# A three-block transformer on one NeuronCore: stage boundaries split by halves of the tokens on both sides

## The reference, cut to what matters

```
block 1, layer 0:  ffn -> mlstm -> ffn -> ple          (each: x = x + f * rms(branch(rms(x)*g)) * g')
block 1, layer 1:  shared k,v from x; ffn -> diff attention -> ffn -> ple
block 2:           x = x + mix(rms(x));  x = x + peer_ffn(rms(x))
block 3:           x = x + rms(mix3(rms(x)));  x = x + rms(ffn3(rms(x)))
def rms_norm(x, gain):
    y = xf * lax.rsqrt(jnp.mean(xf * xf, axis=-1, keepdims=True) + EPS)
```

## Time and profile before

| | |
|---|---|
| runs | 3053.67, 3053.16, 3058.65 us |
| profiled execution, its span | 3052.69 us, 3050.9 us |
| PE busy, matmuls | 2913.1 us (95% of the span), 19486 |
| DVE busy | 1884.8 us (62%) |
| ACT busy | 1568.7 us (51%) |
| mean granted TensorE clock | 0.97 |
| DMA | 490.50 MB, mean 161 GB/s |

### The profile page before, as it was taken

How to read it: one execution, slowest core, us unless ns; L and a number is a source line. 1 busy time by engine, 2 the same in 40 slices (tenths; PEclk the granted TensorE clock), 3 DMA queues, 4 the chain that set the end, 5 groups by cost and what they waited for, 6 DMA issues and landing times.

```text
span 3050.9 us, 46945 instructions
## 1 busy us (share of the span) xinstructions
PE 2913.1 (95%) x19486; PEld 2677.4 (88%) x19486; DVE 1884.8 (62%) x3140; ACT 1568.7 (51%) x2487; POOL 367.4 (12%) x322
## 2 busy tenths in 40 slices
PE   7999899799988997999999999999999999999998
PEld 7978898699768986889998999999888889989996
DVE  4556554645465555767775689677555556655775
ACT  4444444544444445446554444677555555644663
POOL 0000000100000000100000244698000000000000
PEclk9999999899988998999999999999999999999999
DMA  6544455355424553435426454433555564535453
GB/s 200 187 151 148 155 189 191 112 184 188 164 78 142 187 187 135 170 111 160 157 68 196 164 182 172 143 129 138 194 193 193 193 216 132 168 94 180 152 200 125
DMA packets 304228, 490.50 MB, mean 161 GB/s; under 512 B 10816, under 2 KB 236480, under 8 KB 295312
## 3 DMA queue, kind: packets, MB, share of 16 engines
q1 hardware_dynamic: 302880, 480.09, 46.9%
q0 software_dynamic: 1136, 7.41, 0.7%
HBM read 485.36 MB, written 2.10 MB: 160 GB/s over the span
## 4 chain that ended last, share of the span: by engine, by line
PE 88%; DVE 6%; ACT 4%; issue 1%; POOL 1%; DMA 0%; SPq 0%; DVEq 0%; POOLq 0%; ACTq 0%
PE ps L474 30%; PE ps L443 17%; PE ps L444 16%; PE ps L447 16%; PE ps L888 2%; ACT AR L2206 1%; DVE AR L1187 1%; DVE halves L1134 1%; PE ps L922 1%; ACT XH L2191 1%; POOL st L1019 1%; PE ps L425 1%; PE ps L942 1%; DVE AR L1853 1%; DVE AR L1204 0%
## 5 line engine op out<-in xcount | busy, mean ns | idle before, releaser
L2176 ACT ACTIVATE halves<-raw 128x1024 fp32r<-128x1024 f32 (+2 forms) x907 | 950.2, 1053 | 952.9 <-PE ps L447 502.3
L1134 DVE TENSOR_TENSOR halves<-raw,halves 128x1024 fp32r<-128x1024 f32 (+2 forms) x858 | 1031.9, 1218 | 399.3 <-ACT halves L2176 396.8
L443 PE MATMUL ps<-XH,halves 128*128 128x256 f32 x3968 | 999.2, 289 | 7.6 <-DVE XL L1159 4.8
L444 PE MATMUL ps<-XL,halves 128*128 128x256 f32 x3968 | 989.0, 286 | 0.0
L443 PEld LDWEIGHTS ps<-XH,halves 128*128 128x128 f32 x3968 | 771.7, 194 | 14.2 <-DVE XL L1159 6.4
L444 PEld LDWEIGHTS ps<-XL,halves 128*128 128x128 f32 x3968 | 771.8, 194 | 1.0
L447 PE MATMUL ps<-XH,halves 128*128 128x256 f32 x3968 | 561.2, 284 | 1.2 <-DVE halves L1134 1.0
L447 PEld LDWEIGHTS ps<-XH,halves 128*128 128x128 f32 x3968 | 515.4, 193 | 2.5 <-DVE halves L1134 1.8
L474 PE MATMUL ps<-halves,R 128*128 128x512 f32 x1872 | 428.6, 391 | 3.6 <-DVE halves L1134 1.9
L474 PEld LDWEIGHTS ps<-halves,R 128*128 128x128 f32 x1872 | 352.1, 189 | 77.4 <-DVE halves L1134 2.3
L474 PE MATMUL ps<-halves,XH 128*128 128x512 f32 x1600 | 407.4, 393 | 12.4 <-ACT halves L2176 6.6
(11 more groups left out here) (336 smaller groups left out, 2545.7 us busy)
## 6 DMA issues: line engine op xcount, KB each, us to landing
raw<-in_w_ffn_in SPq DMA_DIRECT2D x88, 1024.0 KB, 5.0
raw<-in_w_in SPq DMA_DIRECT2D x74, 1024.0 KB, 5.1
raw<-in_uT SPq DMA_DIRECT2D x64, 1024.0 KB, 4.8
raw<-in_peer_v SPq DMA_DIRECT2D x64, 1024.0 KB, 4.8
raw<-in_w_ffn_out SPq DMA_DIRECT2D x44, 1024.0 KB, 4.8
raw<-in_w_up SPq DMA_DIRECT2D x24, 1024.0 KB, 5.4
raw<-in_mlstm_w_in SPq DMA_DIRECT2D x12, 1024.0 KB, 5.2
raw<-in_w_down SPq DMA_DIRECT2D x12, 1024.0 KB, 4.9
```

What stands on the lines that cost most here:

```text
L443: mm(o, hi[:, q, 0:M], xh[:, k0 + q, :], start=first and q == 0, stop=False)
L444: mm(o, hi[:, q, 0:M], xl[:, k0 + q, :], start=False, stop=False)
L1134: te.tensor_tensor(lo, src, hi.bitcast(F32), ALU.subtract).then_inc(k.lo_made, 1)
L2176: act(hi, src, ACT.Copy).then_inc(k.hi_made, 1)
```

## The change

1. **Products by halves at the start of a stage.** `turn_half` turns one half of the tokens into banks of its own (`main` for half 0, `aux` for half 1, two feature tiles a bank; for `ple` and after the shared keys four tiles a bank). `by_halves` takes the first four pieces, does all four for half 0 (128 columns of XH or XL), calls `second()` (the transposes of half 1), and does all four for half 1. `features` and `gated` use it, `tokens` has its own form (half the 512-column matmuls for each half of the tokens). It stands after in, f00, ml, p0, f10, df, p1, m2, pr and m3.
2. **More pieces kept at the end of a stage.** LATE is a table: 5 for f00, ml, f01, f10, df, f11, m3; 4 for pr; 3 for p0, p1, m2, f3. The kept ones have homes in free parts of AR (`ASIDE`), so that the four homes of the ring already hold the next stage's first four pieces; `upto` says how far ACT and DVE run ahead.
3. **A shorter chain of norms.** ACT squares both sides of 512 (two accumulators), DVE multiplies by the gain row before the power is known (`weighted`), and one scalar_tensor_tensor adds to x. XN is written by ACT (first 512 features) and DVE (the rest) for both halves. The transposed half 0 is taken out of PSUM (`enter(0)`) between the chains of the halves.
4. **Low parts** after a boundary are made on DVE, not on POOL. `small` of mlstm (the gates' rows) comes after `ml.q`, and the transposes of f10 come after `kv.k`.

```diff
+    def turn_half(key, prev, j, banks, per=2):
+        for c0 in range(0, 8, per):
+            b = banks.take(pe, (key, j, c0))
+            pe.wait_ge(*s["xn_high" if c0 < 4 else "xn_low"].need((prev, j)))
+            for c in range(c0, c0 + per):
+                ins = transpose(ps[:, b, (c - c0) * 128:(c - c0) * 128 + 128], k.XN[:, j, c * 128:(c + 1) * 128],
+                                ident[:])
+            filled((key, j, c0), ins)
...
+    def by_halves(outs, act, ready, second):
+        kept = []
+        for j in range(2):
+            if j:
+                second()
+            for i, o in enumerate(outs):
+                if j == 0:
+                    kept.append(weights())
+                n, hi, lo = kept[i]
+                ins = tile_mms(o, n, hi, lo, act, 0, 8, True, True, ready, j=j)
+                if j:
+                    ins.then_inc(k.piece_read, 1)
...
-            mm(o, hi[:, q, 0:M], xh[:, k0 + q, :], start=first and q == 0, stop=False)
-            mm(o, hi[:, q, 0:M], xl[:, k0 + q, :], start=False, stop=False)
+            mm(o[:, ts], hi[:, q, 0:M], xh[:, k0 + q, ts], start=first and q == 0, stop=False)
+            mm(o[:, ts], hi[:, q, 0:M], xl[:, k0 + q, ts], start=False, stop=False)
...
-LATE = 3
+LATE = {"f00": 5, "ml": 5, "f01": 5, "p0": 3, "f10": 5, "df": 5, "f11": 5, "p1": 3, "m2": 3, "pr": 4, "m3": 5, "f3": 3}
...
-    def ffn(key, prev, extra=None):
-        turn(key + ".x", k.XN, normed(prev))
-        if extra:
-            extra()
-        gated(key, 22, turned(key + ".x"))
+    def ffn(key, prev):
+        turn_half(key + ".x", prev, 0, main)
+        gated(key, 22, turned_x(key + ".x"), lambda: turn_half(key + ".x", prev, 1, aux))
         down(key, 22, k.pair(0, 22), hidden(key))
...
@@ vector_engine, residual
+            te.tensor_tensor(XN[:, j, hs], src(j, h), k.gb(slot)[:, hs], ALU.mult) \
...
+                te.scalar_tensor_tensor(x[:, j, hs], XN[:, j, hs], st[:, 26 + j:27 + j], x[:, j, hs], ALU.mult, ALU.add) \
+                    .then_inc(*s["x_sum"].mark((key, j, h)))
...
+            weighted(1, 1)
+        if key not in ("f01", "f11"):
+            enter(0)
+            low_to(k.next_four(key) if more else -1)
+            weighted(1, 0)
...
@@ scalar_engine, residual
+        x_high(0)
+        square(1, 0)
+        if not mid:
+            enter(0)
+            high_to(k.next_four(key) if more else -1)
+        square(1, 1)
...
+    high_to(3)
+    for j in range(2):
+        into["in"](j)
```

More of the change, by code:

```diff
@@ L478, in rows_mm, with tokens @@
         return ins
-    def tokens(key, ncol, act, ready, KT=8, late=False):
+    def tokens(key, ncol, act, ready, KT=8, late=False, second=None):
         for s0 in range(0, ncol, 512):
@@ L483, in tokens @@
             kept = []
+            if second and s0 == 0:
+                for j in range(2):
+                    if j:
+                        second()
+                    for k0 in range(0, KT, 2):
+                        if j == 0:
+                            kept.append(weights())
+                        n, hi, lo = kept[k0 // 2]
+                        ins = rows_mm(bs, n, hi, lo, act, k0, 2, 512, k0 == 0, k0 == KT - 2, ready, (j,), j)
+                        if j:
+                            ins.then_inc(k.piece_read, 1)
+                    if j == 0:
+                        filled((key, s0, 0), ins)
+                k.full[key, s0, 1] = k.piece_read, n + 1
+                continue
             for k0 in range(0, KT, 2):
@@ L535, in small, with gated @@
         k.full[key, "small"] = k.piece_read, m + 1
-    def gated(key, nf, ready):
-        for f in range(0, nf, 2):
+    def gated(key, nf, ready, second=None):
+        kept = []
+        for a in "gu" if second else "":
+            b = main.take(pe, (key, a, 0))
+            for g in range(2):
+                kept.append(ps[:, b, g * 256:g * 256 + 256])
+            k.full[key, a, 0] = k.piece_read, pe.cur + len(kept)
+        if second:
+            by_halves(kept, X, ready, second)
+        for f in range(len(kept) // 2, nf, 2):
             for a in "gu":
@@ L964, in tensor_engine @@
     ple("p0", "f01")
[L965 removed]
+    ffn_kv("f10", "p0")
     diff("f10")
@@ L1034, in second @@
                              (key, "x", j))
[L1036 to L1043 removed]
+        for j in range(2):
+            first(j)
+            second(j)
     def normed(prev):
         for j in range(2):
[L1047 to L1048 removed]
+            gp.wait_ge(*s["xn_low"].need((prev, j)))
             gp.wait_ge(*s["xn_high"].need((prev, j)))
@@ L1244, in tokens @@
             for k0 in range(0, KT, 2):
-                weights(not (late and s0 + 512 == ncol and k0 > 2))
+                weights()
             for j in range(2) if not (late and s0 + 512 == ncol) else ():
@@ L1445, in shared_kv @@
     def shared_kv():
-        turned("kv.x", k.pair(16384, 8), lambda c: col("kv", c))
         features(nothing, "kv.k", 8)
+        half = turned_x("f10.x", X, gain(1, 0), (aux, aux), 4)
+        for j in range(2):
+            half(j)
         tokens(lambda c, j: None, 1024)
@@ L2240, in tokens, with down @@
             for k0 in range(0, KT, 2):
-                weights(not (late and s0 + 512 == ncol and k0 > 2))
+                weights()
             for j in range(2) if not (late and s0 + 512 == ncol) else ():
                 evac(s0, j)
-    def down(key, KT, row, factor, more=True, each=None, mid=nothing):
+    def down(key, KT, row, factor, more=True, each=None, mid=None):
         for t in range(KT):
```

415 lines of the change are left out of this document (254 added, 161 removed), and 4 rows, old and new, of the table ASIDE.

## The result

The changed kernel takes 3170.6 us (median of 4 runs, 3163.2 to 3184.6) against 3054.3 for the kernel before on the same chip: 1.038 times as long (95% interval 1.035 to 1.042). The forecast was 3130. In the profiled execution the span is 3161.4, which is 110.5 more than before, where +76 was forecast.

The account below looks back on a forecast made before the run. It took PE's stream as the bound (work in hand for 95% of the span), so only boundary gaps could be won. Its terms summed to +76 on 3052.7, hence 3130, with its own range 3085 to 3210 (58%), overall 3045 to 3210.

Parts of the forecast that it names:

- Half a piece costs as much as a whole one: First four pieces by halves: 128-column matmuls held to 0.112 us by weight loads, 2.69 us a piece against 2.88.
- A pass: Four half pieces for one token half: 11.0 us, the first piece tile by tile behind ACT and DVE.
- Boundary at full clock: After f00, ml, f10, df, m3: no wait for half 0, second pass ends at +25.6 us; sum +7.6.
- a sign of error: A wait over 2 us ahead of the first transposes after f00, ml, f10, df, m3 would show lead or chain wrong.
- the fourth rival: Half 0 isn't early, low parts on DVE standing ahead of its chain: +10 to +15, inside the first case's range; no chance of its own.
- the term of 12.2: At m2 and pr, two passes ending at 25.1 us against 18.9 and 19.2: +12.2 together.
- Start: PE cold at the program's start, both passes 20.4 us at 1.2 GHz: 63.6 against 34.2, +29.4.
- p0: Behind p0 PE idles 3.8 us, so both passes run at the low clock: 50.8 against 33.0, +17.8.
- The other seven: Remaining boundaries: the clock may fall, 20 us each, bounds 0 and 140; one to two falls taken, +30.
- A pass can't bring a low clock up: Passes of 128-column matmuls begun at 1.2 GHz stay there, 0.213 us a matmul, 20.4 us a pass.
- the one that had the clock hold everywhere: Loads bind, but the clock holds or comes up within passes: 3064, or 3078 at 0.120 a matmul; chance 22%.
- The one with hidden loads: Weight loads hidden in the passes, 0.067 us a matmul, a pass 7.4 us: -55, 2998; chance 15%.

Follow-up runs that it names:

- the experiment with half the weights: Changed kernel, each 128-column matmul of the passes by halves taking 64 of its 128 weight columns, plus eight bank-filling matmuls at the start: 2985.7 us, one run.
- the fillers: Changed kernel plus matmuls that serve nothing on PE at the program's start alone, 20 ahead of the first transposes and 26 behind them: 3186.6 us, one run.
- the second: The changed kernel itself run once more, nothing altered, for a second profiled execution: 3183.5 us, span 3181.7.
- the kernel with fillers: Changed kernel plus matmuls that serve nothing in PE's idle time at the start and every boundary: 3070.9 us, 1.004 times the kernel before.
- the kernel with whole pieces: Changed kernel with first pieces of 256-column projections taking both token halves in one matmul again, the rest kept: 3027.5 us, 0.990 times the kernel before.
- fillers brought 8: Whole-token pieces as in the kernel with whole pieces, plus matmuls that serve nothing in PE's idle time at boundaries and start: 3019.7 us against 3027.5.

## Why the prediction was right and where it was off

- **Half a piece costs as much as a whole one**: right, in size too. 0.112 was forecast and measured, and the experiment with half the weights shows that the load sets it. The Trainium skill's 81 ns for a pair of load and matmul (TensorE: Matmul & The Clock Gate, Back-to-back issue gap) isn't reached by these fp32r weights of 128 columns; rows of another kind of matmul with the same load had it right. The recorded loads would have misled: 195 less 162 ns for 32 columns is 1.03 ns a column and makes 0.13 us, not the 0.11 that I wrote.
- **A pass**: 11.0 forecast, 10.74 and 11.02 measured. The term for a first piece at DVE's pace was not needed: 16 matmuls at 0.112 on eight tiles are as slow as DVE's writes (2.16 for eight).
- **Boundary at full clock**: 25.6 forecast, 25.8 after df, 27.3 after ml. The 1.69 us of waiting there, and the 2.68 after m3, I had at zero, and 2 us was what I had named as a sign of error: at these two the fourth rival holds, low parts on DVE standing ahead of half 0's norm. It is worth some 1.5 and 2.5 us, not 10 to 15. m2 and pr 25.4 (25.1); but the times before were 20.4 and 20.7, so the change costs 9.7 there, and the term of 12.2 was too large, since its two windows before began 1.5 us late (with them set right the forecast sum is +73). p1 20.8 (22.4): it gained 6.8, not 5.2. The chain of half 0 took 6.1 us (6.5).
- **Gates after f01 and f11**: -6 and -5 forecast, -7.0 and -5.9 measured in the stretches that hold them.
- **Start** 63.3 us (63.6). I called PE cold; that is right as far as it goes, but the fillers show that a warm PE falls in the same place if 2 us of idle time stand ahead of the pass. **p0** 48.7 (50.8).
- **The other seven**: this is the term that was too small. One to two falls were forecast, +30; there were three in the first profile (f00, f10, m3) and four in the second. Each cost about the 20 that was worked out (with fillers the stretches that hold the boundaries after f00, f10 and m3 are 21.5, 19.1 and 19.4 shorter, and that after p0, which had a term of its own, 20.7). 110.5 less 76 is 34.5: 30 of it are the one and a half falls too few. The rest is the waits after ml and m3 and single us elsewhere, with both signs. So the prices were right, and how many of the seven would fall was a guess.
- **A pass can't bring a low clock up**: right in all of them. No slow pass in either profile ended faster than it began, and with half the weights it rose 4 to 6 us into the pass.
- **The end**: -1.7 (-1.5).
- **Rivals**: the one that had the clock hold everywhere would have been 3064 to 3078; the kernel with fillers, which makes it hold in 17 of 18 passes, takes 3070.9. So its sum was good and its condition wrong. The one with hidden loads is met by the kernel with half the weights (2985.7). The fourth, that half 0 isn't early, holds in part after ml and m3 alone: PE's wait for ACT went from 62.4 to 12.6 us.

What stays open: why the clock fell behind f00 and f10 in both profiles, and in that with fillers at the start alone, and behind df in none of the three. The gaps ahead of the first pass are 1.63 us at each of these boundaries, and at ml the same gaps gave both outcomes.

## What to carry to other kernels

Splitting a matmul's moving side halves its stream but not its weight load: with 128 fp32r weight columns a 128-column matmul costs 0.112 us against 0.120 for 256 (and at the low clock 0.213 against 0.213), so such a split can hardly pay. Even where half 0's pass runs wholly in idle time, half 1's alone takes 2.69 us a piece against 2.88 for both halves at once: 0.2 a piece to win. That is worked out from these prices; halves of fewer than four pieces were not run. A split in which each half has its own weights (here the activations) is free and won 7.4 us in m2.

Matmuls bound by their loads are also fragile: after idle stretches of 1.3 to 3.6 us the clock fell at some boundaries and stayed down for as long as they lasted, and at the low clock they cost nearly double (0.213). When an early half starts a chain, look at what its follow-up work on ACT and DVE is put ahead of; moving half 0's writes behind half 1's norm was worth 16 us in the kernel with whole pieces, where fillers brought 8.

## What was not expected of the hardware

- A core's first stretch is recorded at a clock of 1.00 while its matmuls run at half that (0.213 us each from 20.48 on; in the kernel with fillers at the start alone the first 12 begin 0.32 us apart, and from the 14th on 0.16).
- One program, with waits equal to 0.01 us, had its clock fall at a boundary in one execution and not in another, and 20 us hung on it. A single profile of such a kernel is one throw of the dice.
- The same 128-column matmul with 64 columns of weights starts every 0.060 us, close to one column a cycle (0.053).
